# Pooling layer of a six-layer forward pass: two of the three products through one loaded weight tile

## The reference

```
u = rms_norm(h, norm_g)                       # (256, 1024)
xb, z = split(u @ w_in, 2)                    # w_in: (1024, 4096), xb and z: (256, 2048)
for g, window in enumerate((2, 4, 8, 16)):    # four groups of 512 features
    pooled[g] = mean of xb[:, g] over the last window tokens - xb[:, g]
mixed[g] = pooled[g] @ w_group[g]             # (512, 512) each
y = mixed * scale * silu(z)
h = h + y @ w_out                             # w_out: (2048, 1024)
```

## Time and profile before

| | |
|---|---|
| median of 3 runs | 927.43 us (925.85 to 927.92) |
| profiled execution, its time | 925.88 us |
| profiled execution, its span | 924.2 us |
| granted TensorE clock, mean | 0.999 of 2.4 GHz |
| PE busy | 903.8 us, 98% |
| VectorE busy | 648.6 us, 70% |
| ScalarE busy | 499.8 us, 54% |
| GpSimd busy | 299.6 us, 32% |
| unit x0 ends, by the next waits | about 552.1 us |
| mix3 ends | about 656.2 us |
| last out unit ends | about 702.6 us |

### The profile page before, as it was taken

The page is one execution under the profiler, slowest core; times in us unless marked ns, Lnnn a source line. Parts: engine busy times, 40 slices in busy tenths (PEclk is TensorE's granted clock), DMA queues, the critical chain, the costliest instruction groups (busy, mean ns, idle before and its releaser), DMA issues.

```text
span 924.2 us, 16528 instructions
## 1 busy us (share of the span) xinstructions
PE 903.8 (98%) x6625; PEld 843.3 (91%) x6625; DVE 648.6 (70%) x1022; ACT 499.8 (54%) x730; POOL 299.6 (32%) x243
## 2 busy tenths in 40 slices
PE   8999999999999999989999999999999999999997
PEld 8999997788879998779999999999999997989886
DVE  5886666889885789866776676988637554656642
ACT  5644445654865658875444453353535336676742
POOL 8433323383111323113333208975103000122320
PEclk9999999999999999999999999999999999999999
DMA  9996536334414433445786435444673653343431
GB/s 248 231 228 183 182 105 225 126 134 164 171 62 151 144 101 134 132 123 140 185 227 203 171 132 207 148 139 176 234 270 101 246 201 103 116 159 117 158 114 45
DMA packets 123584, 148.69 MB, mean 161 GB/s; under 512 B 9561, under 2 KB 79102, under 8 KB 123518
## 3 DMA queue, kind: packets, MB, share of 16 engines
q1 hardware_dynamic: 121472, 145.63, 48.9%
q10 hardware_dynamic: 1582, 1.12, 0.4%
q0 software_dynamic: 464, 1.02, 0.4%
HBM read 146.70 MB, written 1.05 MB: 160 GB/s over the span
## 4 chain that ended last, share of the span: by engine, by line
PE 66%; DVE 8%; ACT 4%; POOL 1%; issue 1%; POOLq 0%; ACTq 0%; DVEq 0%
PE acc L1785 48%; PE aux L1785 17%; DVE wlo L947 2%; DVE wlo L968 1%; ACT work L705 1%; POOL sqy L1699 1%; ACT work L707 1%; DVE work L1286 1%; ACT work L720 1%; PE aux L2157 1%; DVE arena L1055 0%; DVE sqy L1146 0%; DVE hf L1156 0%; ACT whi L491 0%; ACT arena L748 0%
## 5 line engine op out<-in xcount | busy, mean ns | idle before, releaser
L947 DVE TENSOR_TENSOR wlo<-raw,whi 128x2048 fp32r<-128x2048 f32 (+5 forms) x114 | 273.6, 2422 | 82.0 <-ACT whi L483 80.1
L1785 PE MATMUL acc<-xh,whi 128*128 128x256 f32 x1128 | 321.8, 285 | 1.2 <-ACT arena L748 0.6
L1785 PE MATMUL acc<-xh,wlo 128*128 128x256 f32 x1128 | 319.1, 283 | 0.0
L1785 PE MATMUL acc<-xl,whi 128*128 128x256 f32 x1128 | 319.1, 283 | 0.0
L483 ACT ACTIVATE whi<-raw 128x2048 fp32r<-128x2048 f32 (+5 forms) x115 | 197.9, 1746 | 89.3 <-PE acc L1785 51.4
L1785 PEld LDWEIGHTS acc<-xh,whi 128*128 128x128 f32 x1128 | 215.9, 191 | 3.3 <-issue 1.6
L1785 PEld LDWEIGHTS acc<-xl,whi 128*128 128x128 f32 x1128 | 216.0, 192 | 0.0
L1785 PEld LDWEIGHTS acc<-xh,wlo 128*128 128x128 f32 x1128 | 215.9, 191 | 0.0
L1785 PE MATMUL acc<-whi,xh 128*128 128x512 f32 (+1 forms) x208 | 81.4, 391 | 1.6 <-DVE arena L1055 0.5
L1785 PE MATMUL acc<-whi,xl 128*128 128x512 f32 (+1 forms) x208 | 78.8, 379 | 0.0
L1785 PE MATMUL acc<-wlo,xh 128*128 128x512 f32 (+1 forms) x208 | 78.8, 379 | 0.0
(11 more groups left out here) (349 smaller groups left out, 1738.3 us busy)
## 6 DMA issues: line engine op xcount, KB each, us to landing
raw<-in_a_w_in SPq DMA_DIRECT2D x52, 512.0 KB, 6.7
raw<-in_sb_w_in SPq DMA_DIRECT2D x48, 512.0 KB, 5.5
raw<-in_b_w_in SPq DMA_DIRECT2D x36, 512.0 KB, 5.4
raw<-in_pool_w_in SPq DMA_DIRECT2D x32, 512.0 KB, 5.6
raw<-in_a_w_out SPq DMA_DIRECT2D x16, 512.0 KB, 4.9
raw<-in_pool_w_out SPq DMA_DIRECT2D x16, 512.0 KB, 5.8
raw<-in_sb_w_out SPq DMA_DIRECT2D x16, 512.0 KB, 5.0
raw<-in_b_w_out SPq DMA_DIRECT2D x8, 512.0 KB, 4.8
```

Source lines behind the costliest of these rows:

```text
L947: TT(wlo[b][:, lo:hi], (raw_third if third else raw[b])[:, lo:hi], whi[b][:, lo:hi].bitcast(F32), ALU.subtract).then_inc(lo_ready, 1)
L1785: return nc.tensor.matmul(out_, lhsT, rhs, start=start, stop=stop, skip_group_check=True)
```

## The change

In units 0 to 9 (`WHOLE_BANKS`) one product streams high and low data, 2 x 256 columns, past the high weights into a whole bank: columns 0 to 255 hold high by high, 256 to 511 high by low. A second product of 256 columns, low weights by high data, is added to the first half. For this `xh` and `xl` become the two parts of one tensor `xhl`, and `ph` and `pl` of `phl`, at the same places in memory. A unit now fills four banks, `acc` and `aux` by turns. The two halves are added behind it: ScalarE copies the second halves of the four banks to `pool_sum` (128 x 1024, at the place of `work`), and VectorE adds the first halves to them (`pool_halves`). For x and z the sum is written to its place and then multiplied by `r` there; for a mix it is written back to `pool_sum`, from which the gating reads. TensorE waits for `pool_freed` of unit i-2, ScalarE's copy waits until VectorE has read the last one. Units 10 and 11 stay as they were. Since the factors `r` come to VectorE through `aux`, unit 1 waits for `r_taken` ahead of that bank; it takes its tiles in the order 2, 3, 0, 1.

```diff
-        xh, xl = put("xh", [P, NK, T], F32R), put("xl", [P, NK, T], F32R)
+        xhl = put("xhl", [P, 2, NK, T], F32R)
+        xh, xl = xhl[:, 0, :, :], xhl[:, 1, :, :]
...
-        ph = at("ph", [P, 4, T], F32R, arena_at + 31 * tile_bytes)
-        pl = at("pl", [P, 4, T], F32R, arena_at + 35 * tile_bytes)
+        phl = at("phl", [P, 2, 4, T], F32R, arena_at + 31 * tile_bytes)
+        ph, pl = phl[:, 0, :, :], phl[:, 1, :, :]
...
+        pool_sum = at("pool_sum", [P, 4, T], F32, work_at)
...
+        WHOLE_BANKS = 10
...
             for i, (kind, g) in enumerate(POOL_UNITS):
+                if i < WHOLE_BANKS:
+                    act.wait_ge(unit_done, P0 + i + 1)
+                    if i:
+                        act.wait_ge(sem("pool_freed"), i)
+                    if i and POOL_UNITS[i - 1][0] == "mix":
+                        act.wait_ge(sem("y_ready"), 32 + POOL_UNITS[i - 1][1] + 1)
+                    A(pool_sum[:, :, :], (acc, aux)[i % 2][:, :, T:2 * T], ACT.Copy).then_inc(sem("xl_part"), 1)
...
-            spread_copy(4)
+            spread_copy(4, taken="r_taken")
+            rb4 = r[:, :].rearrange("p (n t) -> p n t", n=1).broadcast_to([P, 4, T])
+
+            def pool_halves(i, dst):
+
+                bank = (acc, aux)[i % 2]
+                dve.wait_ge(sem("xl_part"), i + 1)
+                TT(dst, bank[:, :, 0:T], pool_sum[:, :, :], ALU.add).then_inc(sem("pool_freed"), 1)
+                dve.wait_ge(sem("pool_freed"), i + 1)
...
                 if kind == "x":
                     if g:
                         dve.wait_ge(sem("pooled"), g)
-                    for c in range(2):
-                        ins = TT(pad[0][:, 2 * c:2 * c + 2, mid], psum[c], rb, ALU.mult)
-                        ins.then_inc(sem("xb_taken"), 1)
+                    xb = pad[0][:, :, mid]
+                    pool_halves(i, xb)
+                    TT(xb, xb, rb4, ALU.mult).then_inc(sem("xb_taken"), 2)
                     split(P0 + i + 2)
                 elif kind == "z":
...
-                    for c in range(2):
-                        ins = TT(arena[:, 39 + 2 * c:41 + 2 * c, :], psum[c], rb, ALU.mult)
-                    ins.then_inc(sem("z_raw"), 1)
+                    z = arena[:, 39:43, :]
+                    if i < WHOLE_BANKS:
+                        pool_halves(i, z)
+                        TT(z, z, rb4, ALU.mult).then_inc(sem("z_raw"), 1)
...
                 else:
+                    if i < WHOLE_BANKS:
+                        pool_halves(i, pool_sum[:, :, :])
                     dve.wait_ge(sem("z_ready"), g + 1)
                     for n in range(4):
                         c = G_PS + 4 * ORDER[g] + n
-                        ins = STT(arena[:, 39 + n, :], acc_tile(i % 2, n), G[:, c:c + 1], arena[:, 39 + n, :],
-                                  ALU.mult, ALU.mult)
+                        ins = STT(arena[:, 39 + n, :], pool_sum[:, n, :] if i < WHOLE_BANKS else acc_tile(i % 2, n),
+                                  G[:, c:c + 1], arena[:, 39 + n, :], ALU.mult, ALU.mult)
...
+            def pool_unit(u, i, both, before=None):
+
+                K, C = unit_shape(u)
+                wh, wl = w_view(u, K, C)
+                bank = (acc, aux)[i % 2]
+                for k in range(K):
+                    if k in (0, K // 2):
+                        pe.wait_ge(lo_ready, 2 * u + 1 + (k > 0))
+                    if before:
+                        before(k)
+                    for n in (2, 3, 0, 1):
+                        if i == 1 and k == 0 and n == 1:
+                            taken("r_taken", 1)
+                        c = slice(P * n, P * n + P)
+                        mm(bank[:, n, :].rearrange("p (a t) -> p a t", a=2), wh[:, k, c], both[:, :, k, :], k == 0)
+                        ins = mm(bank[:, n, 0:T], wl[:, k, c], both[:, 0, k, :], False)
+                ins.then_inc(unit_done, 1)
+
             for i, (kind, g) in enumerate(POOL_UNITS):
-                if i >= 2:
...
+                if 2 <= i < WHOLE_BANKS + 2:
+                    taken("pool_freed", i - 1)
```

More of the change, by code:

```diff
@@ L1033, in factor, with spread_copy @@
                     spread_copy(m, square)
-            def spread_copy(m, square=False):
+            def spread_copy(m, square=False, taken=None):
                 dve.wait_ge(sem("r_psum"), m + 1)
                 me.link(V.tensor_copy(r[:, :], aux[:, 1, 0:T]))
+                if taken:
+                    dve.sem_inc(sem(taken), 1)
                 if square:
@@ L1489, in _ @@
                         dve.wait_ge(sem("yl_ready"), 32 + g)
-                    for c in range(2):
-                        ins = TT(arena[:, 39 + 2 * c:41 + 2 * c, :], psum[c], rb, ALU.mult)
-                    ins.then_inc(sem("z_raw"), 1)
-                else:
+                    z = arena[:, 39:43, :]
+                    if i < WHOLE_BANKS:
+                        pool_halves(i, z)
+                        TT(z, z, rb4, ALU.mult).then_inc(sem("z_raw"), 1)
+                    else:
+                        for c in range(2):
+                            ins = TT(arena[:, 39 + 2 * c:41 + 2 * c, :], psum[c], rb, ALU.mult)
+                        ins.then_inc(sem("z_raw"), 1)
+                else:
+                    if i < WHOLE_BANKS:
+                        pool_halves(i, pool_sum[:, :, :])
                     dve.wait_ge(sem("z_ready"), g + 1)
@@ L2264, in pool_first @@
                     spread(4)
+            def pool_unit(u, i, both, before=None):
[14 more added lines that the diff above has]
+                ins.then_inc(unit_done, 1)
             for i, (kind, g) in enumerate(POOL_UNITS):
-                if i >= 2:
-                    kind2, g2 = POOL_UNITS[i - 2]
-                    taken(*{"x": ("xb_taken", 2 * g2 + 2), "z": ("z_raw", 4 + g2 + 1),
-                            "mix": ("y_ready", 32 + g2 + 1)}[kind2])
+                if 2 <= i < WHOLE_BANKS + 2:
+                    taken("pool_freed", i - 1)
                 if kind == "mix":
                     taken("pl_ready", g + 1)
-                unit(P0 + i, in_tiles(i % 2), *((ph, pl) if kind == "mix" else (xh, xl)),
-                     pool_first if i == 0 else None)
+                if i < WHOLE_BANKS:
+                    pool_unit(P0 + i, i, phl if kind == "mix" else xhl, pool_first if i == 0 else None)
+                else:
+                    unit(P0 + i, in_tiles(i % 2), *((ph, pl) if kind == "mix" else (xh, xl)))
             for h in range(3):
```

## The result

The changed kernel takes 940.85 us (median of 4 runs, 940.03 to 941.25) against 927.35 of before, measured beside it (4 runs, 925.85 to 927.92): 13.5 us more, a ratio of 1.015, 95% interval 1.0137 to 1.0162. The forecast was 940.5 (930 to 948), slower.

What follows compares the result with a forecast made beforehand. TensorE, busy 98%, was taken to bound the kernel, with VectorE nearly full beside it. Waits of 17.0 less TensorE's 3.3 us gave +13.7, so 941.1 from the median 927.43; forecast 940.5, range 930 to 948.

Steps and rivals of the forecast that it cites:

- What bounds the kernel: Whole kernel: TensorE, busy 98% of the span; beside it, whether VectorE, ScalarE and GpSimd prepare the next unit in time.
- the margin at mix 0: Behind mix 0: the next unit's first low half is ready only 0.3 us before the mix ends.
- The blocked price for the moved operand: Mix's four VectorE products from pool_sum: each waits for a GpSimd operation, about 2.4 us instead of 0.47.
- Rival A: Mix's four products out of pool_sum: not blocked by GpSimd; +8 us, 935.5; chance 0.2.
- The addition out of PSUM not blocked: VectorE's additions of the two halves: 1.22 us each, whatever GpSimd does.
- Rival B: VectorE's addition of PSUM and pool_sum: blocked by GpSimd too; +20.7 us, 948; chance 0.13.
- ScalarE's copy: Ten copies of 128x1024 from PSUM ahead of ScalarE's splits: 1.10 us each.
- TensorE's step: Ten whole-bank units: a 512 and a 256 column product take 0.348 us instead of 0.36; -3.3 us in all.
- The walk's waits: TensorE's waits in the pooling layer, walked forward from x1's end: six, 17.0 us in sum, 7.3 the longest before x2.
- The copy of r: VectorE's copy of r out of aux, ahead of unit 1's fourth tile: 0 to 0.5 us, with 0 taken.
- rival C: TensorE behind the long wait: clock falls to 1.2 GHz, 1.4 us lost, 942; chance 0.25 on top of the forecast.

Runs made afterwards that it cites:

- e1: The changed kernel with the mix sums written back to PSUM, where the four gating products read them instead of from pool_sum; 933.86 us, ratio 1.0079.
- e2: The changed kernel with the 512 column product taken apart into 256 column products, the reading of two halves kept; 941.65 us, ratio 1.0155.
- e3: The changed kernel without ScalarE's copy and the addition, only first halves read (high weights by low data missing from the result); 924.70 us, ratio 0.9979.
- e5: The changed kernel with 46 unused products of 256 columns filling TensorE's wait before unit x2; 938.07 us, ratio 1.0124.
- e8: e1 with ScalarE's copy made for unit x0 alone, nine units adding stale pool_sum (part of the result missing); 930.03 us, ratio 1.0042.
- e9: e1 with ScalarE's copy for units x1, x2 and x3 moved ahead of the Silu of the z unit before; 934.56 us, ratio 1.0079.

## Why the prediction was right, step by step

- **What bounds the kernel, and the margin at mix 0**: right. With whole banks in two units, ahead of that margin, the stretch is 0.9 us longer; with four it is 8.4.
- **The blocked price for the moved operand**: right, and it decided the case. Four products in 8.11 us, from 586.94 to 595.05; 12.4 to 20.5 after x1's end; the walk had them between 13.2 and 21.8. Rival A is e1's state, 7.0 us below the changed kernel by the medians; its walk said 5. The Trainium skill ("SBUF — State Buffer", section "SBUF: two separate sides") calls the shared port an exclusive lock that whichever starts first holds for its whole instruction. The trace agrees: the product at 592.48 starts just behind GpSimd's and takes 2.58 us, and none of the twelve takes less than 0.47.
- **The addition out of PSUM not blocked**: right, 1.21 to 1.23 in all ten cases, also at 585.69 beside GpSimd's additions. Rival B falls. VectorE's waits for its own addition, put under 0.1 each without a row, are 0.04 to 0.11.
- **ScalarE's copy**: 1.00 to 1.03, forecast 1.10. Its consequences were larger than its length: without nine of them 3.1 us go.
- **TensorE's step**: right to the ns that shows: four pairs from 605.33 to 606.72 are 0.348 each. Its 3.3 in the sum are consistent, as the waits beside it were walked with the shorter units; but e2 shows that without the saving the time would be only 0.75 longer, and e3 that even alone it brings 0.9 to 2.0.
- **The walk's waits**: right in place and order, too long in size. Forecast 2.0, 7.3, 0.7, 3.3, 1.5, 2.2 (17.0); the rows have 1.69, 6.12, 0.55, 2.28, 1.18, 1.48 (13.3). A row counts from the modelled end of the last product; by starts each wait is 0.16 longer (record 0.28, step 0.12), 14.3 in all. The walk had GpSimd take every turn; in the trace mix 0's last product (the gating's, on VectorE) ended 20.5 after x1's end (574.5) instead of 21.8.
- **The copy of r**: put at 0 in a range of 0 to 0.5, it is 0.28, plus 0.1 for the slower product behind it.
- **The clock, rival C**: it came true on top of the forecast, at 0.25. Its price was 1.4 with an end at 5.6; it is 2.6. The mis-sized term is the time at half clock: taken from 16 products of 128 columns at the program's start, where the trace of after has nine pairs. The Trainium skill ("TensorE: Matmul & The Clock Gate", section "Part 1: The HAM clock gate (the "warmup" mystery)") has activity release the throttle; e5, where only activity was added, agrees.

The mechanism was right; that the total came so near was luck, since two errors cancelled: waits 2.7 too long and a clock loss of 2.6 left out. (The prediction's own sum gave 941.1; for the 940.5 it has no working.) The sum of what was measured, 14.3 + 2.6 + 0.3 - 3.3 = 13.9, meets the 14.07 of the stretch.

## What to carry to other kernels

When an edit moves an operand of VectorE from PSUM to SBUF, look up what GpSimd does in those microseconds before you price it: here the same product took 0.47 or 2.6 us. In this kernel a saving on the busiest engine wasn't worth its full size, because the engines that feed it didn't have that much room. Walk the loop with all engines from the narrowest margin, and read first what stands behind it in the queue of the engine that gets the new work. And where the walk gives TensorE a wait of some microseconds, price the clock behind it too: 2.6 us here behind 6.12, 1.6 behind 2.03 and 2.28, where it fell at all.

## Not expected of the hardware

The length of a wait alone didn't tell whether the clock falls. After 2.28 us the changed kernel went on at full clock (633.38 above, first record 0.47; window 633 to 635 at 1.00), as e8 did after 2.19. e9 stood for the same 2.28 us at another place and lost 1.6 us: five pairs from 615.76 to 619.10 (TensorE's row and a window).

```profile
615.76 0.77 PE L1818 MATMUL aux<-xhl,whi 128*128 128x512 f32 x1 [2.28 <-DVE wlo L963]
```
```profile
616.00:618.00 2.00, 2.00 (x7) 1.72 (x8) 2.00 (x1) 0.35 (x1) 1.92 (x2) 0.50 0.00 0
```

In e1 the clock fell after 2.03 (0.63 in 606 to 608). What tells these apart stays open.
